# The first recurrent layer in another unit order: four recurrence column blocks and the gate matrices ahead of three of the four GELU blocks, and the convolution's low halves on VectorE

## What is computed

```python
def recurrent_block(x, w_in, conv_w, conv_b, w_gate, b_gate, lam, w_out):
    u = x @ w_in
    gate, rec = u[..., :D_RNN], u[..., D_RNN:]
    rec = causal_depthwise_conv(rec, conv_w, conv_b)
    h = rg_lru(rec, w_gate, b_gate, lam)
    return (jax.nn.gelu(gate) * h) @ w_out
```

## Time and profile before

| | us |
|---|---|
| three runs, median (lowest, highest) | 1095.55 (1095.34, 1096.88) |
| the profiled execution's time | 1094.01 |
| its span | 1092.1 |
| TensorE busy | 1037.0 (95%) |
| VectorE, ScalarE, GpSimd busy | 652.5, 567.1, 120.1 |

### The profile page before, as it was taken

How to read it: one execution, slowest core, us unless ns; L and a number is a source line. 1 busy time by engine, 2 the same in 40 slices (tenths; PEclk the granted TensorE clock), 3 DMA queues, 4 the chain that set the end, 5 groups by cost and what they waited for, 6 DMA issues and landing times. The chain is left out here.

```text
span 1092.1 us, 16410 instructions
## 1 busy us (share of the span) xinstructions
PE 1037.0 (95%) x6694; PEld 929.1 (85%) x6694; DVE 652.5 (60%) x881; ACT 567.1 (52%) x854; POOL 120.1 (11%) x118
## 2 busy tenths in 40 slices
PE   5887999999999989999999989999999979999997
PEld 5886799999988856699899979988899869999996
DVE  5658675555567755575555564365654657676764
ACT  6586464444446455464444454455544356556652
POOL 3555110000000011330000000000001510000000
PEclk9999999999999969999999999999999989999999
DMA  9643567555545431375556527543344625655520
GB/s 314 197 155 123 185 225 238 192 177 190 175 138 205 163 108 39 121 231 192 189 192 192 181 94 226 173 136 117 101 131 131 216 78 193 196 190 193 193 78 38
DMA packets 117970, 180.40 MB, mean 165 GB/s; under 512 B 3113, under 2 KB 93577, under 8 KB 117913
## 3 DMA queue, kind: packets, MB, share of 16 engines
q1 hardware_dynamic: 116099, 174.16, 48.7%
q0 software_dynamic: 1696, 5.39, 1.5%
q10 hardware_dynamic: 118, 0.05, 0.0%
HBM read 178.48 MB, written 1.10 MB: 164 GB/s over the span
## 5 line engine op out<-in xcount | busy, mean ns | idle before, releaser
L996 PE MATMUL PS<-XA,whi 128*128 128x256 f32 x2576 | 473.1, 286 | 8.2 <-DVE XA L1472 5.0
L1421 DVE TENSOR_TENSOR wlo<-raw,whi 128x2048 fp32r<-128x2048 f32 x153 | 351.5, 2304 | 170.4 <-ACT whi L605 166.1
L996 PEld LDWEIGHTS PS<-XA,whi 128*128 128x128 f32 x2576 | 407.2, 193 | 18.7 <-issue 14.5
L605 ACT ACTIVATE whi<-raw 128x2048 fp32r<-128x2048 f32 x158 | 301.4, 1912 | 148.4 <-PE PS L1041 117.5
L996 PE MATMUL PS<-XA,wlo 128*128 128x256 f32 x1288 | 366.4, 284 | 0.0
L996 PEld LDWEIGHTS PS<-XA,wlo 128*128 128x128 f32 x1288 | 248.8, 193 | 0.0
L1041 PE MATMUL PS<-whi,XB 128*128 128x512 f32 x800 | 226.7, 391 | 1.0 <-DVE XB L1683 1.0
L1041 PEld LDWEIGHTS PS<-whi,XB 128*128 128x128 f32 x800 | 147.6, 188 | 29.9 <-issue 1.7
L1041 PE MATMUL PS<-wlo,XB 128*128 128x512 f32 x400 | 127.5, 390 | 0.0
L1041 PEld LDWEIGHTS PS<-wlo,XB 128*128 128x128 f32 x400 | 75.2, 188 | 15.8
L1041 PE MATMUL PS<-whi,XA 128*128 128x512 f32 x256 | 73.7, 396 | 10.0 <-DVE XA L1553 8.4
(11 more groups left out here) (207 smaller groups left out, 1013.2 us busy)
## 6 DMA issues: line engine op xcount, KB each, us to landing
raw<-in_w_up SPq DMA_DIRECT2D x32, 1024.0 KB, 5.5
raw<-in_w_down SPq DMA_DIRECT2D x32, 1024.0 KB, 4.9
raw<-in_w_ffn_up SPq DMA_DIRECT2D x22, 1024.0 KB, 5.1
raw<-in_w_in SPq DMA_DIRECT2D x21, 1024.0 KB, 5.2
raw<-in_w_ffn_down SPq DMA_DIRECT2D x11, 1024.0 KB, 4.9
raw<-in_a_w_in SPq DMA_DIRECT2D x8, 1024.0 KB, 8.5
raw<-in_w_kv SPq DMA_DIRECT2D x8, 1024.0 KB, 6.1
raw<-in_w_mem_kv SPq DMA_DIRECT2D x4, 1024.0 KB, 5.2
```

Of the source, the lines that this page charges most:

```text
L605: act.activation(whi[:, s, :], raw[:, s, :], ACT.Copy).then_inc(s_hi, 1)
L996: ins = pe.matmul(PS[:, bank_of(g), 0:T], w[:, k, P * m:P * m + P], X[:, k0 + k, part, :], start=(i == 0 and part == 0 and w is hi), stop= ...
L1421: dve.tensor_tensor(wlo[:, s, :], raw[:, s, :], whi[:, s, :].bitcast(F32), ALU.subtract).then_inc(s_lo, 1)
```

## The change

Units are renumbered: 0 to 3 are the record columns, 4 the first gate unit, 5 the gate matrices, 6 to 8 the other gate units; 9 and up are as before. TensorE takes them in that order, with the transposes of `mem` (`norm_T(1)`) between units 6 and 7. ScalarE no longer applies GELU while it copies gate groups out: `gate_out` copies, and two GELU instructions of 128x1024 follow at the end. The decay (`decay(h)`) comes in two halves, before and after the first copy-out of a gate unit behind the sigmoids, ahead of `norm_hi(1)`; `s_ew` is waited for ahead of `rec_unit(2)`. VectorE makes the convolution's low halves (`conv_lo`) in place of GpSimd, takes over the low halves of units 12 to 15, and runs root arguments, scans and products between its weight splits. GpSimd keeps the norm's roots and the two products with i.

```diff
-U_REC, U_GATE, U_LRU = [0, 1, 3, 5], [2, 4, 6, 7], 8
+U_REC, U_GATE, U_LRU = [0, 1, 2, 3], [4, 6, 7, 8], 5
...
-G_REC, G_GATE, G_MEMK = [0, 2, 6, 10], [4, 8, 12, 14], 16
+G_REC, G_GATE, G_MEMK = [0, 2, 4, 6], [8, 10, 12, 14], 16
...
     gate_ = [cols(a_in, KT, 256 * i) for i in range(4)]
-    w_units += [rec[0], rec[1], gate_[0], rec[2], gate_[1], rec[3], gate_[2]]
-    w_units += [gate_[3], A["a_w_gate"][0].rearrange("k p n -> p k n")]
+    w_units += rec + [gate_[0], A["a_w_gate"][0].rearrange("k p n -> p k n")] + gate_[1:]
...
-        POOL_SPLIT_MEM = [u + LEAD for u in range(U_MEMK, U_MEMV + 2)]
...
             pool.dma_start(bias_rows[16:32, :], erow[0:16, 1, :]).then_inc(s_ew, 16)
-            for k in range(KT):
-                if k == KT - 2:
-                    roots(SQ_NORM[1])
-                pool.wait_ge(s_ch, k + 1)
-                pool.tensor_tensor(XB[:, k, 1, :], xc[:, k, :], XB[:, k, 0, :].bitcast(F32), ALU.subtract)\
-                    .then_inc(s_cl, 1)
+            roots(SQ_NORM[1])
...
                 pool.tensor_tensor(v, v, xc[:, 4 * h:4 * h + 4, :], ALU.mult).then_inc(s_ix, 1)
-            for u in POOL_SPLIT_MEM:
-                split(u)
...
-            def gate_unit(i):
-                unit_a(U_GATE[i], G_GATE[i], [gate[:, 2 * i + m, :] for m in range(2)], ACT.Gelu_apprx_tanh)
+            def gate_out(i):
+                for m in range(2):
+                    evac(G_GATE[i] + m, BEFORE(U_GATE[i]) + m + 1, gate[:, 2 * i + m, :])
+            def decay(h):
+                act.wait_ge(s_lru, 8)
+                act.wait_ge(s_cc, 1)
+                for n in range(4 * h, 4 * h + 4):
+                    act.activation(av[:, n, :], rg[:, n, :], ACT.Exp, scale=cneg[:, n:n + 1]).then_inc(s_a, 1)
+                for n in range(4 * h, 4 * h + 4):
+                    act.activation(rg[:, n, :], rg[:, n, :], ACT.Tanh, scale=cpos[:, n:n + 1]).then_inc(s_a, 1)
...
             act.wait_ge(s_ew, 32)
-            gate_unit(0)
+            rec_unit(2)
             conv_hi(1)
-            rec_unit(2)
-            gate_unit(1)
+            rec_unit(3)
...
             squares(SQ_NORM[1], xn, lambda i: act.wait_ge(s_mem, 16))
-            rec_unit(3)
-            gate_unit(2)
+            split(U_GATE[0] + LEAD)
             conv_hi(3)
-            gate_unit(3)
+            gate_out(0)
...
             split(U_LRU + LEAD)
+            decay(0)
+            split(U_GATE[1] + LEAD)
+            gate_out(1)
+            decay(1)
             norm_hi(1, [(XB, R_MEM)], bank=4)
-            split(U_MEMK + LEAD)
-            act.wait_ge(s_lru, 8)
-            act.wait_ge(s_cc, 1)
-            for h in range(2):
-                for n in range(4 * h, 4 * h + 4):
-                    act.activation(av[:, n, :], rg[:, n, :], ACT.Exp, scale=cneg[:, n:n + 1]).then_inc(s_a, 1)
-                for n in range(4 * h, 4 * h + 4):
-                    act.activation(rg[:, n, :], rg[:, n, :], ACT.Tanh, scale=cpos[:, n:n + 1]).then_inc(s_a, 1)
-                for m in range(2):
-                    evac(G_MEMK + 2 * h + m, BEFORE(U_MEMK + h) + m + 1, kT_me[:, 2 * h + m, :])
+            split(U_GATE[2] + LEAD)
+            gate_out(2)
...
                 act.activation(rg[:, 4 * h:4 * h + 4, :], rg[:, 4 * h:4 * h + 4, :], ACT.Sqrt).then_inc(s_sq, 1)
-            split(U_MEMK + 1 + LEAD)
+            split(U_GATE[3] + LEAD)
+            gate_out(3)
+            for h in range(2):
+                v = gate[:, 4 * h:4 * h + 4, :]
+                act.wait_ge(s_evac, G_GATE[2 * h + 1] + 2)
+                act.activation(v, v, ACT.Gelu_apprx_tanh).then_inc(s_gelu, 1)
+            for h in range(2):
+                split(U_MEMK + h + LEAD)
+                for m in range(2):
+                    evac(G_MEMK + 2 * h + m, BEFORE(U_MEMK + h) + m + 1, kT_me[:, 2 * h + m, :])
...
             pe.matmul(PS[0:16, 7, 0:384], relb[0:32, :], onehot[0:32, :], start=True, stop=True).then_inc(s_eps, 1)
-            unit_a(U_REC[1], G_REC[1])
-            for i in range(2):
-                unit_a(U_GATE[i], G_GATE[i])
-                unit_a(U_REC[2 + i], G_REC[2 + i])
-            unit_a(U_GATE[2], G_GATE[2])
-            unit_a(U_GATE[3], G_GATE[3])
+            for i in range(1, 4):
+                unit_a(U_REC[i], G_REC[i])
+            unit_a(U_GATE[0], G_GATE[0])
...
                 ins.then_inc(s_step, 1)
+            unit_a(U_GATE[1], G_GATE[1])
...
             norm_T(1, bank=4)
+            unit_a(U_GATE[2], G_GATE[2])
+            unit_a(U_GATE[3], G_GATE[3])
...
                 dve.wait_ge(s_hi, it * units + u + 1)
-                if u - 1 in POOL_SPLIT_MEM + POOL_SPLIT_O:
+                if u - 1 in POOL_SPLIT_O:
...
-            split(U_REC[0] + LEAD)
-            conv(0)
-            split(U_REC[1] + LEAD)
-            conv(1)
-            for i in range(2):
-                split(U_GATE[i] + LEAD)
-                split(U_REC[2 + i] + LEAD)
-                conv(2 + i)
+            def conv_lo(i):
+                for k in (2 * i, 2 * i + 1):
+                    dve.wait_ge(s_ch, k + 1)
+                    dve.tensor_tensor(XB[:, k, 1, :], xc[:, k, :], XB[:, k, 0, :].bitcast(F32), ALU.subtract)\
+                       .then_inc(s_cl, 1)
+            for i in range(4):
+                split(U_REC[i] + LEAD)
+                conv(i)
+                if i:
+                    conv_lo(i - 1)
+            split(U_GATE[0] + LEAD)
+            conv_lo(3)
             norm(1, xn, [])
-            split(U_GATE[2] + LEAD)
-            split(U_GATE[3] + LEAD)
+            split(U_LRU + LEAD)
...
-            norm_lo(1, [(XB, R_MEM)], bank=4, late=U_LRU + LEAD)
-            for h in range(2):
+            def scale2(h):
...
-            dve.wait_ge(s_evac, G_GATE[3] + 2)
-            for h in range(2):
+            def scan(h):
...
                 link(dve.tensor_tensor(half(ig, h), half(ig, h), half(rg, h), ALU.mult))
-                if h == 1:
-                    y_lo(0)
...
+            def y_out(h):
+                dve.wait_ge(s_gelu, h + 1)
...
+            scale2(0)
+            split(U_GATE[1] + LEAD)
+            scale2(1)
+            norm_lo(1, [(XB, R_MEM)], bank=4, late=U_GATE[2] + LEAD)
+            scan(0)
+            split(U_GATE[3] + LEAD)
+            scan(1)
+            dve.wait_ge(s_step, AFTER[U_GATE[3]])
+            for h in range(2):
+                y_out(h)
+            split(U_MEMK + LEAD)
+            y_lo(0)
+            split(U_MEMK + 1 + LEAD)
+            split(U_MEMV + LEAD)
...
             dve.tensor_copy(v_me[:], PS[:, 0:2, :]).then_inc(s_bev, 1)
+            split(U_MEMV + 1 + LEAD)
```

## The result

The kernel after takes 1085.37 us (median of 4 runs, 1084.73 to 1087.79), the kernel before beside it 1096.22 (1095.34 to 1097.11): a ratio of 0.9905, 95% interval 0.9887 to 0.9923. The forecast was 1088.0, with a range from 1085.5; the sign was right, the gain 10.85 us where 7.5 was expected, and the median lies 0.13 us under the range. The profiled execution took 1085.35 us with a span of 1083.4.

What follows compares the result with a forecast made beforehand. TensorE was taken as the bound, gaining only where it waits, chiefly before `U_ROUT`. An earlier start (5.6 us) plus no slow restart (1.9) gave 7.5 off 1095.55: 1088.0, own range 1087 to 1089, wider range 1085.5 to 1091.5.

Steps and rivals of the forecast that it cites:

- The cause: Recurrence: GpSimd's weight splits hold off VectorE's first-half scans (6.81 against 2.43 us) and product (5.33 against 1.23).
- The rival that gave them to the operations themselves: Recurrence: long VectorE rows are not GpSimd's doing, so `U_ROUT` starts 2.4 us later, about 1098; chance 0.04.
- Part 1: ScalarE's queue from 40.83 to unit 9: no gaps, sigmoids done at 61.7, unit 7's first copy at 81.0.
- Part 2: TensorE in units 4 to 8: new 4.4 us wait for the first sigmoid in unit 5, then low clock.
- the term of 1.6: Unit 5's blocks 4 to 7 at low clock delay the last sigmoid and ScalarE's queue by 1.6 us.
- Part 3: Unit 9 to the MLP: `U_ROUT` starts 5.6 us earlier, at 105.1, without idle; its slow restart saves another 1.9.
- Part 4: Moved and added work, including the convolution's low halves on VectorE: no cost; `s_ew` delay taken as 0.
- The rule of the drain: ScalarE table switches: each costs 1.4 us more than its load, giving 1090.8 to 1093.6; chance 0.03.
- the clock did not hold: Rival at 56 us in unit 5: the clock holds, the 1.6 us falls away, giving 1086.4; chance 0.22.
- the ties were not late: Rival at units 11 and 12: thin margins slip by one to three us, giving 1089 to 1091; chance 0.16.
- the wait did not only move: Rival: the earlier idle time returns at units 5 and 9, giving 1092 to 1095; chance 0.07.
- The baseline: The forecast gain was subtracted from the runs' median, 1095.55, not from the profiled execution's 1094.0.

Runs made afterwards that it cites:

- a1: Kernel before, old unit order, with only the four low halves of units 12 to 15 moved from GpSimd to VectorE: 1090.33 us, 0.9940 of before.
- a2: Kernel after with the four low halves of units 12 to 15 given back to GpSimd: 1096.6 us, 0.9987 of before.
- b1: Kernel after, unchanged, run once more: 1087.25 us, 0.9905 of before.
- b4: Kernel after with VectorE's last two convolution low halves moved ahead of the low half of unit 7's weights: one run, 1087.46 us.
- a3: Kernel after with the convolution's eight low halves given back to GpSimd: 0.9912 of before.
- c1: Kernel after with ScalarE's tables' wait late, squares early, copy-outs of units 7, 9, 10 ahead of splits, VectorE's unit 12 low half ahead of output: 1079.20 us, 0.9832.
- d1: c1 with unit 8's copy-out also moved ahead of ScalarE's split of unit 11: 1079.18 us, 0.9839 of before.
- c2: Kernel after with the low halves of units 12 to 15 on GpSimd, each as four shorter instructions: 1090.24 us, 0.9935 of before.

## Why the prediction was right, and where it was off

**The cause was right and is shown.** The long scans and products were GpSimd's doing: a1 alone brings them to their short times and gains 6.6 us, and a2 takes nearly all of the gain away. The rival that gave them to the operations themselves (1098) is out.

**Part 1, ScalarE's chain**, held: the table load is at 54.27 (forecast 54.5), the sigmoids end at 61.7 (61.7), the first copy of unit 7 at about 80.4 (81.0 before the shift).

**Part 2 holds the step that failed.** The release by the first sigmoid was forecast at 56.5 and came at 56.55; the wait was forecast at 4.4 and was 2.5, or 4.0 in b1 and b4, since the clock may fall once before. What was mis-sized is the last sentence: blocks 4 to 7 wholly at the low clock, 5.8 us, the last sigmoid 1.6 later, and "ScalarE's whole queue shifts by 1.6". In b1, where the clock fell just there, TensorE goes from block 4 (56.52) to unit 6 (60.95) in 4.4 us, because the clock is back before the blocks end, and the sigmoids end at 62.0. The shift is 0.3, and in the kernel after it is nothing (61.7). a2, whose program is the same up to here, kept the low clock longer: 5.3 us for the blocks, the last sigmoid at 62.8, a shift of 1.2. The first matmuls of unit 6 in b1, then in a2:

```profile
60.95 0.40 PE L999 MATMUL PS<-XA,whi 128*128 128x256 f32 x2
```
```profile
61.77 0.63 PE L1002 MATMUL PS<-XA,whi 128*128 128x256 f32 x2
```

So the term of 1.6 measured 0 to 1.2 from execution to execution; even wholly at the low clock a block's six matmuls take 1.3 us and not 1.4. Unit 9 started at 80.50 (80.83 in b1) where 82.6 was forecast: 1.6 of the shift and 0.5 of sums on the high side.

**Part 3** held as a difference: unit 9 to `U_ROUT` 22.6 us (22.5), no wait in front of it, and its slow restart gone, since `U_ROUT` to the MLP is 22.65 us where it was 24.61. That is 1.96 (1.9). So `U_ROUT` came 2.0 us earlier than forecast, and nearly all of that is part 2's shift.

**Part 4** was half right. VectorE makes a pair of low halves in 0.76 us (0.8), but "no cost" missed a gain. I had read one engine's holding-off of the other at the scans and had not asked for it at the convolution, where GpSimd's low halves stood before. a3 shows 1.0 us of it in unit 5, and 1.6 to 2.0 at `U_ROUT`, of which a part may be the clock's; the runs alone cannot confirm it. `s_ew` was free (40.90 for 40.83).

**The rule of the drain** does not hold here: the load at 54.27 takes 1.28, and the sigmoids begin at 55.57. Of the other rivals, the clock did not hold (two low stretches), the ties were not late, and the wait did not only move, though in c1 it did just that.

**The baseline.** 7.5 was taken off a median of 1095.55. Between the profiled executions the gain is 8.66, between the medians 10.85, and b1's 1087.25 beside 1097.14 gives the same 0.9905. The profiled execution of before (1094.01) is 1.3 us under the fastest of its four timed runs (1095.34), so the trace explains 2.0 us more than the forecast at the MLP and does not show where the rest of the difference between the medians lies. The level moved by 1 to 2 us between the two sessions of these kernels, and the ratio did not. A lower end of 1085.5 was too near for that.

## What to carry to other kernels

Before giving VectorE help from GpSimd, look where GpSimd's instructions will lie: a VectorE row that is long in one place and short in another for the same work was, in this kernel, standing and not working. Long GpSimd instructions belong where VectorE is idle, or are cut in pieces if what they make is not urgent. A wait that stands early in an in-order queue should be moved down to the first instruction that needs it (here worth more than half as much as the whole change). After an edit that frees one engine, look whether the copy-outs that the next one needs stand behind long work: moving them took the last wait out of the trace in d1, though the runs do not show a gain.

## What the hardware showed that was not expected

- VectorE lost 12.9 us to 15.4 us of GpSimd's work, and 5.2 us when the same work came in quarters. A row of the profile counts that standing as busy time.
- The clock's fall is not fixed by the length of a wait in this range: 2.0 us at 43.7 was followed by 0.50 in one execution, 2.3 us at the same place in b1, with the same program, was followed by 1.00. Nor is the length of the low stretch: behind the same wait of 4.0 us at 56.5 the clock was back at 59.9 in b1 and at 62.5 in a2. At unit 9 the three executions lie 1.2 us apart (80.50, 80.83, 81.66).
- The releaser that the profile names for a wait can be the wrong one of two: VectorE's low half in after, b1, a2 and c2, the sigmoid in b4, at the same moment within 0.1 us.
